# Twelve row slots for two expert tables: four and eight in place of five and seven

## The chip, the cores and the metric

The kernel runs on one core of one Trainium2 chip. The metric is the device time in microseconds of one execution.

## What is computed

Two transformer-like blocks run one after the other on a sequence of 256 tokens of width 1024, all in float32. The part that matters here is the end of the first block, a layer of small experts. For every token and each of 8 heads, a router picks 16 of 16384 experts, so 128 a token; expert k of a token has one row of 1024 numbers in table u and one in table v:

```
def expert_chunk(args):
    xc, ic, gc = args
    u = jnp.take(u_tab, ic, axis=0)
    a = jnp.einsum('chkd,cd->chk', u, xc)
    wgt = gc * jax.nn.gelu(a)
    vv = jnp.take(v_tab, ic, axis=0)
    return jnp.einsum('chk,chkd->cd', wgt, vv)
```

Everything ahead of it (modulation, attention over a window, a short convolution, an output projection) and the whole second block (a state-space mixer, a matrix memory, a feed-forward layer) is untouched by the change.

## The kernel before, in words

**Tiles.** The 256 tokens are two tiles of 128, one token to a partition. The expert layer is a flat sequence of 256 steps, which the text calls experts 0 to 255: 128 for the first tile and 128 for the second. Step e gathers, for each of the 128 tokens, the u row and the v row of that token's expert e: two indirect DMAs of 128 rows of 4 KB, 512 KB each.

**The slots.** The buffer `G` (tile name `gathered`, 12 x 1024 columns) is cut at line 372 into NU + NV = 12 slots: the first NU take u rows in turn (`e % NU`), the other NV take v rows (`e % NV`). NU = 5 and NV = 7 stand in lines 70 and 71. Each slot has a semaphore for its landing (lines 444 and 445). Before the expert layer, other parts of `G` hold attention buffers and a chunk of the output projection's weights (from column 8192 on).

**Who does what.** Five engines work on the steps, each in its own order:

- POOL issues the gathers, in the order u 0, v 0, u 1, then for every e from 1 on u(e + 1), v(e) (lines 678 to 711). `gather_u` waits at line 686 until the dot that last used the slot is done, `gather_v` at line 696 until the pair of sums that holds the slot's last user is done. Sums are counted in pairs: `pairs(n)` is `(n + 1) // 2`, and PE counts only behind every odd expert. POOL works its queue in order, so a u gather that waits also holds up the v gathers behind it, and the other way round.
- DVE multiplies the u row with the token's activation and adds up (`dot_expert`, line 2489, one instruction of 1024 columns), then drains and counts `dot_ready` (line 2491). Between the dots it works through the routing of the experts to come, one piece a step (`route_piece`): it picks the best keys, makes the indices and the gate values of the next 32 experts. A piece can wait for scores that ACT copies out of PSUM.
- ACT makes the weight of the step (`weigh_expert`, lines 1737 to 1746): gelu of the dot, times the gate, spread over a diagonal of 128 x 128. There are 8 diagonals, so expert e waits for the pair with expert e - 8. ACT also copies scores (line 1563) and other PE results in between.
- PE multiplies the diagonal with the v row and adds into two PSUM banks (`sum_expert`, line 1143, two halves of 512 columns, which the profile shows as four matmul records), and has other matmuls laid in between at fixed experts: queries and scores for the router (lines 780 and 1069), and the first products of the second block.
- SP loads weights for these other matmuls.

After expert 255, POOL adds some bias rows and the second block runs.

Of the kernel before, what the change touches and what calls it, by code (L numbers as in the profile page):

```python
# [66 lines left out]
UP_PLACE = {1: (0, 0), 6: (0, 1), 2: (1, 0), 5: (1, 1), 3: (2, 0), 7: (2, 1), 4: (3, 0)}  # L67
UP_BANKS = 4
LAST_PRODUCTS = (1, 6, 2, 5, 3, 7, 4)
NU = 5  # L70
NV = 7
ACC = 4
ROUTE = 2 * TOPK
EXPERTS = HEADS * TOPK
# [170 lines left out]
def pairs(experts):  # L245

    return (experts + 1) // 2


def build(nc, T, out):  # L250

    with ExitStack() as ctx:
# [3 lines left out]
        def sem(name):  # L256
            return ctx.enter_context(nc.semaphore(name))
# [113 lines left out]

        rows = G[:, :].rearrange("p (s n) -> p s n", s=NU + NV)
        u_rows, v_rows = rows[:, 0:NU, :], rows[:, NU:NU + NV, :]
        h2_rows = [psum[:, b:b + 2, :].rearrange("p b n -> p (b n)") for b in H2_BANK]
# [68 lines left out]
        turn_read = sem("turn_read")  # L443
        u_full = [sem(f"u_full{i}") for i in range(NU)]
        v_full = [sem(f"v_full{i}") for i in range(NV)]
        S_ = {}

        def flag(name):

            if name not in S_:  # L450
                S_[name] = sem(name)
            return S_[name]
# [89 lines left out]
        def route_step(e):  # L542

            return e // TOPK if e < ROUTE else e // ROUTE + 1
# [91 lines left out]
        def _(pool):  # L636
# [41 lines left out]
            def gather_u(e):  # L678

                r, k, slot = e // ROUTE, e % ROUTE, e % NU  # L680
                if e in FIRST_IDX:
                    pool.wait_ge(flag("idx_ready"), FIRST_IDX.index(e) + 1)
                elif e == TOPK or (k == 0 and r):
                    pool.wait_ge(flag("idx_ready"), route_step(e) + len(FIRST_IDX))
                if e >= NU:
                    pool.wait_ge(flag("dot_ready"), e - NU + 1)
                pool.indirect_dma_start(  # L687
# [4 lines left out]
            def gather_v(e):  # L692

                r, k, slot = e // ROUTE, e % ROUTE, e % NV
                if e >= NV:
                    pool.wait_ge(flag("pair_summed"), pairs(e - NV + 1))
                if e == 0:
# [2483 lines left out]
```

## Time and profile before

| | us |
|---|---|
| median of 3 runs | 1310.25 |
| lowest and highest of them | 1309.9, 1311.06 |
| span of the profiled execution | 1366.9 |
| time of the profiled execution itself | not given beside its span |
| POOL busy in the span | 500.2 |
| DVE busy | 861.8 |
| PE busy | 1199.9 |

The profile was taken in an execution of its own, which is longer than the runs without one. Times are microseconds from the start of the span. A row of the timeline has the start, the duration, the engine, the line of the kernel, the operation and its tiles, and in brackets how long the engine was idle before it and what ended that. "issue" is idle time that waited for nothing the profile shows, "remote" a releaser that is not on record. DVEq is the sequencer of DVE, which counts a drain. The busy time of POOL holds the issuing of the indirect DMAs, not their transfers.

### The profile page before, as it was taken

The page shows a single profiled execution, that of the slowest core. Times are in us where ns is not written, and L with a number is a line of the kernel's source. Part 1 is how long each engine was busy: PE and PEld are TensorE (multiplying, and loading weights), DVE is VectorE, ACT ScalarE, POOL GpSimd, SP SyncE. Part 2 cuts the span into 40 slices and gives each one's busy share as a digit, 9 for nine tenths or more (in the row PEclk, how much of TensorE's full clock was granted, in tenths as well). Part 3 has the DMA queues.
Part 4 walks back from the last instruction along what each step waited for, and adds up shares of the span by engine and source line. Part 5 has one row for each costly group of instructions (what it writes and reads, how often), then busy time and mean ns, then how long its engine had stood idle before and what let it go on. Part 6 is the DMA issues. An engine that isn't in the chain of part 4 may idle for free. (4 is left out here: it accounts for less than half of the span.)

```text
span 1366.9 us, 14592 instructions
## 1 busy us (share of the span) xinstructions
PE 1199.9 (88%) x4663; PEld 665.4 (49%) x4663; DVE 861.8 (63%) x1765; ACT 420.2 (31%) x1138; POOL 500.2 (37%) x580
## 2 busy tenths in 40 slices
PE   7899888888778978876788889789999999999997
PEld 4676554433344542222345433236544545999443
DVE  2657669574663654776746557679989543676345
ACT  2213334344223343343423324432323311222000
POOL 1000356666665666766666666630000000000000
PEclk9999999999998999999999999999999999999999
DMA  9998789999998999999999999986644444454450
GB/s 358 390 349 326 286 319 339 367 357 367 364 366 300 406 403 405 407 377 364 340 371 353 400 405 409 377 306 233 224 139 148 145 150 156 157 175 145 175 184 31
DMA packets 134303, 405.66 MB, mean 297 GB/s; under 512 B 10153, under 2 KB 11585, under 8 KB 133971
## 3 DMA queue, kind: packets, MB, share of 16 engines
q0 software_dynamic: 75024, 273.19, 53.1%
q1 hardware_dynamic: 57860, 127.48, 25.8%
q10 hardware_dynamic: 1342, 4.06, 0.8%
q8 instruction: 38, 0.62, 0.2%
q14 instruction: 39, 0.31, 0.1%
HBM read 403.12 MB, written 1.05 MB: 296 GB/s over the span
## 5 line engine op out<-in xcount | busy, mean ns | idle before, releaser
L1143 PE MATMUL psum<-gathered,modr 128*128 128x512 f32 x1024 | 505.0, 633 | 130.3 <-DMA gathered<-in_peer_v_dram,expert_idx 49.0
L2489 DVE CUSTOM_DVE_ANT_0 gathered<-gathered,psum 128x1024 f32<-128x1024 f32 x256 | 311.5, 1217 | 202.3 <-DMA gathered<-in_peer_u_dram,expert_idx 153.3
L1143 PEld LDWEIGHTS psum<-gathered,modr 128*128 128x128 f32 x1024 | 190.7, 199 | 404.7 <-issue 284.9
L687 POOL DMA_INDIRECT gathered<-in_peer_u_dram,expert_idx x256 | 244.9, 957 | 240.5 <-DVE expert_idx L1997 144.0
L701 POOL DMA_INDIRECT gathered<-in_peer_v_dram,expert_idx x256 | 242.6, 947 | 169.9 <-remote 73.7
L780 PE MATMUL psum<-featT,weight_ring 128*128 128x128 f32 (+2 forms) x960 | 145.3, 305 | 14.4 <-issue 11.3
L780 PEld LDWEIGHTS psum<-featT,weight_ring 128*128 128x128 f32 x960 | 133.7, 196 | 43.9 <-issue 35.6
L780 PE MATMUL psum<-weight_ring,featT 128*128 128x512 f32 x336 | 147.9, 596 | 1.3 <-ACT featT L1563 0.8
L1737 ACT ACTIVATE gel<-dots 128x1 f32<-128x1 f32 x256 | 51.1, 200 | 255.1 <-issue 128.1
L1746 ACT ACTIVATE modr<-ident,wgt 128x128 f32<-128x128 f32 x256 | 102.8, 402 | 18.5 <-issue 1.1
L780 PEld LDWEIGHTS psum<-weight_ring,featT 128*128 128x128 f32 x336 | 62.6, 190 | 78.8 <-issue 76.6
L1741 ACT ACTIVATE wgt<-gel,expert_gate 128x1 f32<-128x1 f32 x256 | 75.4, 294 | 17.9 <-issue 0.3
L1989 DVE TENSOR_TENSOR work<-work 128x1088 f32<-128x1088 f32 (+5 forms) x87 | 68.6, 801 | 9.6 <-issue 2.8
L725 POOL DMA_DIRECT2D gathered<-in_b_in_dram x6 | 5.3, 942 | 138.6 <-ACT gathered L1585 104.2
L1585 ACT COPY work<-psum 128x128 f32<-128x128 f32 x32 | 8.4, 262 | 81.5 <-remote 44.6
L1978 ACT ACTIVATE work<-work,pack 128x256 f32<-128x256 f32 x28 | 12.7, 500 | 56.8 <-DVE work L1989 56.8
L1989 DVE TENSOR_TENSOR vectors<-weight_ring 128x1024 f32<-128x1024 f32 x14 | 16.5, 1220 | 20.9 <-PE psum L1512 20.9
L1563 ACT COPY featT<-psum 128x512 f32<-128x512 f32 (+1 forms) x24 | 12.4, 554 | 55.0 <-PE psum L752 53.8
L780 PE MATMUL psum<-weight_ring,uT 128*128 128x512 f32 x64 | 28.2, 593 | 1.0 <-ACT gathered L1585 1.0
L1989 DVE TENSOR_TENSOR gathered<-gathered,psum 128x256 f32<-128x256 f32 (+1 forms) x17 | 8.6, 511 | 29.8 <-PE psum L780 24.9
L1473 PE MATMUL psum<-featT,weight_ring 128*128 128x128 f32 x224 | 27.3, 275 | 0.0
L1473 PEld LDWEIGHTS psum<-featT,weight_ring 128*128 128x128 f32 x224 | 26.1, 192 | 0.0
(443 smaller groups left out, 1343.1 us busy)
## 6 DMA issues: line engine op xcount, KB each, us to landing
weight_ring<-in_w_in_dram SPq DMA_DIRECT2D x16, 2048.0 KB
weight_ring<-in_w_up_dram SPq DMA_DIRECT2D x8, 2048.0 KB
weight_ring<-in_w_down_dram SPq DMA_DIRECT2D x8, 2048.0 KB
weight_ring<-in_ada_w_dram SPq DMA_DIRECT2D x5, 2048.0 KB
work<-in_ada_w_dram SPq DMA_DIRECT2D x5, 2048.0 KB, 16.3
weight_ring<-in_peer_wq_dram SPq DMA_DIRECT2D x3, 2048.0 KB
gathered<-in_ada_w_dram SPq DMA_DIRECT2D x2, 2048.0 KB, 14.5
gathered<-in_peer_u_dram,expert_idx POOLq DMA_INDIRECT x256
```

Source lines behind the costliest of these rows:

```text
L687: pool.indirect_dma_start(u_rows[:, slot, :], None, T["peer_u"], bass.IndirectOffsetOnAxis(ap=expert_idx[:, r % 2, k:k + 1], axis=0),).the ...
L701: pool.indirect_dma_start(v_rows[:, slot, :], None, T["peer_v"], bass.IndirectOffsetOnAxis(ap=expert_idx[:, r % 2, k:k + 1], axis=0),).the ...
L780: last = pe.matmul(psum[0:m, bank, 0:n], lhs(k), rhs(k), start=(k == 0), stop=(k == kt - 1))
L1143: mm = pe.matmul(psum[:, SUM_BANK + half, :], diag[:, e % 8, :], v_rows[:, slot, 512 * half:512 * (half + 1)], start=(e % EXPERTS == 0), s ...
L1473: last = pe.matmul(psum[:, UP_BANKS * (n % 2) + bank, at:at + P], a(g, m), b(g), start=(g == 0), stop=(g == 3))
L1563: ins = act.activation(dst, src, func, **kw) if func else act.copy(dst, src)
L1737: act.activation(gel[:, col:col + 1], dots[:, col:col + 1], ACT.Gelu_apprx_tanh)
L1741: act.activation(wgt[:, col:col + 1], gel[:, col:col + 1], ACT.Copy, scale=expert_gate[:, r % 2, k:k + 1])
L1746: act.activation(diag[:, e % 8, :], ident[:, :], ACT.Copy, scale=wgt[:, col:col + 1]).then_inc(flag("diag_full"), 1)
L1978: act.activation(ffT[:, k, :], ffT[:, k, :], ACT.Relu, bias=pk("b_up")[:, k:k + 1])
L1989: return dve.tensor_tensor(o, a, b, op)
L2489: dve.tensor_tensor_reduce(u_rows[:, slot, :], u_rows[:, slot, :], h2_rows[t], 1.0, 0.0, ALU.mult, ALU.add, dots[:, col:col + 1])
```

## The change

The twelve slots are divided four to eight. Nothing else is edited: lines 372, 373, 444, 445, 680, 685, 686, 694 to 696, 1139, 1140, 2485 and 2488 take NU and NV from these two lines.

```
--- before
+++ after
-NU = 5
-NV = 7
+NU = 4
+NV = 8
```

## Rows read from the trace of the kernel before

**Rows 1.** The head of the page

```profile
span 1366.9 us, 14592 instructions
```

**Rows 2.** Windows: us; busy of PE, PEld, DVE, ACT, POOL; PEclk, DMA share, GB/s

```profile
152.00:915.00 763.00, 620.92 (x1844) 298.17 (x1843) 479.45 (x1156) 282.56 (x880) 487.48 (x513) 0.95 0.97 370
...
520.00:580.00 60.00, 51.23 (x103) 18.42 (x102) 38.99 (x102) 21.60 (x70) 40.62 (x43) 0.94 1.03 408
```

**Rows 3.** DMA view, 152 to 915 us: the gathers' queue, packets, MB, share

```profile
q0 software_dynamic: 73728, 268.47, 92.4%
```

**Rows 4.** Timeline, 606 to 617 us: POOL's pace and expert 153

```profile
606.24 0.94 POOL L687 DMA_INDIRECT gathered<-in_peer_u_dram,expert_idx  x1 [0.30 <-issue]
...
608.82 0.94 POOL L687 DMA_INDIRECT gathered<-in_peer_u_dram,expert_idx  x1 [0.30 <-issue]
...
610.07 0.94 POOL L701 DMA_INDIRECT gathered<-in_peer_v_dram,expert_idx  x1 [0.30 <-issue]
...
612.90 1.15 DVE L2489 CUSTOM_DVE_ANT_0 gathered<-gathered,psum 128x1024 f32<-128x1024 f32 x1
...
616.66 1.98 PE L1143 MATMUL psum<-gathered,modr 128*128 128x512 f32 x4 [0.58 <-issue]
```

**Rows 5.** Waits view, POOL: waited for, us in total, times, longest us

```profile
POOL gathered L701 <- remote: 73.7, 29, 4.2
...
POOL gathered L701 <- PE psum L1143: 28.7, 12, 8.7
...
POOL gathered L687 <- DVEq L2491: 23.6, 27, 4.4
```

**Rows 6.** Timeline of POOL, 514 to 535 us: one u gather of the backlog

```profile
527.35 0.94 POOL L687 DMA_INDIRECT gathered<-in_peer_u_dram,expert_idx  x1 [0.38 <-DVEq L2491]
```

**Rows 7.** Timeline: POOL (v 13, v 15, u 17, u 22) and DVE, start

```profile
196.16 0.94 POOL L701 DMA_INDIRECT gathered<-in_peer_v_dram,expert_idx  x1 [1.86 <-PE psum L1143]
...
203.16 0.94 POOL L701 DMA_INDIRECT gathered<-in_peer_v_dram,expert_idx  x1 [2.34 <-PE psum L1143]
...
204.41 0.94 POOL L687 DMA_INDIRECT gathered<-in_peer_u_dram,expert_idx  x1 [0.30 <-issue]
...
218.79 0.94 POOL L687 DMA_INDIRECT gathered<-in_peer_u_dram,expert_idx  x1 [0.30 <-issue]
...
204.52 0.87 DVE L2338 MAX8 work<-work 128x8 f32<-128x128 f32 x4 [9.80 <-ACT work L1563]
...
206.44 0.08 DVE L2489 DVE_READ_ACCUMULATOR2_ANT dots<- 128x1 f32 x1
...
220.55 0.08 DVE L2489 DVE_READ_ACCUMULATOR2_ANT dots<- 128x1 f32 x1
...
251.59 1.22 DVE L2489 CUSTOM_DVE_ANT_0 gathered<-gathered,psum 128x1024 f32<-128x1024 f32 x1 [1.80 <-DMA gathered<-in_peer_u_dram,expert_idx]
```

**Rows 8.** Timeline: POOL (u 88, v 87); two holds of ACT

```profile
408.88 0.94 POOL L687 DMA_INDIRECT gathered<-in_peer_u_dram,expert_idx  x1 [0.30 <-issue]
...
418.52 0.94 POOL L701 DMA_INDIRECT gathered<-in_peer_v_dram,expert_idx  x1 [8.70 <-PE psum L1143]
...
260.50 0.59 ACT L1563 COPY work<-psum 128x512 f32<-128x512 f32 x1 [9.42 <-remote]
...
413.04 0.59 ACT L1563 COPY work<-psum 128x512 f32<-128x512 f32 x1 [15.08 <-remote]
```

**Rows 9.** Timeline of POOL (u 144, v 143) and DVE around 583 us

```profile
580.37 0.93 POOL L687 DMA_INDIRECT gathered<-in_peer_u_dram,expert_idx  x1 [0.30 <-issue]
...
583.55 0.93 POOL L701 DMA_INDIRECT gathered<-in_peer_v_dram,expert_idx  x1 [2.25 <-issue]
...
583.39 0.20 DVE L2384 CAST work<-work 128x64 f32<-128x64 uint32 x1 [4.09 <-issue]
```

**Rows 10.** Timeline of POOL, u 167 and u 168

```profile
645.92 0.94 POOL L687 DMA_INDIRECT gathered<-in_peer_u_dram,expert_idx  x1 [0.30 <-issue]
...
651.76 0.94 POOL L687 DMA_INDIRECT gathered<-in_peer_u_dram,expert_idx  x1 [3.66 <-DVEq L2491]
```

## The prediction

> **What bounds the kernel now.** First the page's head, for the span [rows 1]. The change touches only the stretch in which the two expert tables are gathered, from POOL's first gather at 152 us to the end of the sums near 915 us, so the windows view comes second. In the stretch POOL is busy for 487 of 763 us, DVE for 479, PE for 621, and the DMA engines' share is 0.97 at 370 GB/s; from 520 to 580 us it is 1.03 at 408 GB/s [rows 2]. The reader is to see that no engine is full, that the DMA engines nearly are, and that they can do a tenth more than their mean.
>
> Third, the DMA view: the gathers' queue moves 268.47 MB in the stretch [rows 3]. At 408 GB/s that is 658 us, and one expert (a u row and a v row of 512 KB, 1.05 MB) takes 2.57 us. Fourth, POOL's rows in order of time. A gather holds POOL for 0.94 us and 0.30 us passes before the next, 1.24 us a gather and 2.49 us an expert [rows 4]; 256 experts are 637 us. The rest of the stretch is in POOL's waits: 23.6 us for DVE in front of u gathers (27 times), 28.7 us for PE in front of v gathers (12 times), 73.7 us in which no releaser is on record (29 times) [rows 5]. 637 + 126 is 763; less the 0.30 us counted twice 68 times (20 us) it is 743, and the stretch's last 10 us lie behind the last gather. So POOL's queue sets the pace of the stretch, the DMA engines stand 3% behind it, and a us that POOL is held is a us at the end, except where the DMA engines have a backlog (520 to 580 us: POOL waits 0.38 us for every u slot there [rows 6], and this costs nothing).
>
> The sum is made against one profiled execution with a span of 1366.9 us [rows 1]; the page gives no other time for it. The median of the runs is 1310.25 us, 56.6 us less, so some holds of the trace are surely smaller in the runs, above all those without a releaser. I keep the terms in microseconds and set them on 1310.25.
>
> **The change, part by part.** No instruction is added or removed, and no byte: the same 512 gathers in the same order, 12 slots of the same size, 12 semaphores. Two waits of POOL move. Line 686: u row e waits for dot e-4 in place of e-5. Line 696: pairs(e - 7) in place of pairs(e - 6); for even e both are the pair (e-8, e-7), for odd e it is the pair (e-8, e-7) in place of (e-6, e-5). So every u gather may start one expert (about 2.5 us) less ahead, every odd v gather two experts further ahead, and an even one no further. The v slots move down by 1024 columns; the wait of v 3 for the w_out chunk stays at v 3, where POOL does not wait now; cost nothing, covered by the 0.30 us pace.
>
> Regular flow. Expert 153 [rows 4]: u issued at 606.24, its dot ends at 612.90 + 1.15 = 614.05, 7.8 us later; v issued at 610.07, its sum ends at 618.64, 8.6 us. Five u slots allow 5 x 2.49 = 12.4 us, four 9.96: the slack of a u slot falls from 4.6 to 2.1 us. The odd v row has 6 x 2.49 = 14.9 us now, slack 6.4; with eight slots 7 for even and 8 for odd rows, slack 8.9 at least. While no engine is late both are covered: cost 0. If that cover goes (a dot over 2.1 us late), POOL is held, and v gathers queued behind the u gather, so PE too, are late next. The trade is thus in the holds, and I walk through those of the trace.
>
> (a) Start. POOL counted from its first gather: v 15 waits for PE until 203.16 and u 17 follows at 204.41. With eight v slots v 15 would need only the pair (6, 7), for whose sum v 13 waited until 196.16, and could go at the pace near 199.4; but u 17 then waits for dot 13, which DVE ends at 206.5 after a hold of 9.80 us on the scores [rows 7]. u 17 goes at 206.7, 2.3 us later. Following this on to u 22: it needs dot 18, over at 220.6, and goes at 220.8 in place of 218.79. Cost **+2.0 us**. Is it taken up? At 251.59 DVE stands 1.80 us waiting for a u row [rows 7], so lateness of the stream reaches the dots. Bounds: 0 (taken up by a later hold of POOL) and 2.49.
>
> (b) v 87. ACT is held 15.08 us, until 413.04, the diagonal of expert 81 and its sum are late, and v 87 goes at 418.52 after 8.70 us [rows 8]. With eight slots v 87 needs only the pair (78, 79), a pair earlier than the one that is late: it goes 1.24 us behind u 88 (408.88), at 410.1, u 89 at 411.4, and v 88 waits until 418.5. Two gathers pass before the hold in place of after it: **-2.49 us**. This is the most that one hold on the v side can give.
>
> (c) u 144. DVE is held 4.09 us behind dot 140, until 583.39. u 144 went at 580.37, with four slots it goes at 583.5; v 143, held until 583.55 now, goes at 584.7, the next u at 586.0 in place of 584.8 [rows 9]: **+1.2 us**. Bounds 0 and 2.49.
>
> (d) u 167. u 168 waits 3.66 us for DVE's end of dot 163, until 651.76; with four slots u 167, issued at 645.92 now, is the one that waits [rows 10]. Two gathers fall behind the hold: **+2.5 us** (to 2.9 while DMA restarts).
>
> I counted the other u gathers whose dot e-4 ends after their present issue: they lie in e 4 to 12 and 17 to 24 (in a), at 37 and 38 (1.4 us, inside the 2.0 already carried), and in the stretches in which the DMA engines have a backlog (e 106 to 137, 209 to 212, 224 to 232), where a later issue costs nothing as DMA is full.
>
> Sum: 2.0 - 2.49 + 1.2 + 2.5 = **+3.2 us**; 1310.25 + 3.2 = 1313.4. Nothing behind 915 us changes but its start. With every bound at its low end the sum is -2.49 + 0 + 0 + 0 = -2.5, at its high end without (b) it is 2.49 + 2.49 + 2.9 = +7.9.
>
> A page against this sum: the Trainium skill, "DMA: Bandwidth & Descriptors", section Specifications, gives about 358 GB/s as the limit of one core's HBM reads. By it the gathers alone would take 750 us, the stretch would be bound by bytes, and the change would give 0. The 408 GB/s over 60 us [rows 2] speaks against it here, with one core running.
>
> **The rivals.** *No change.* If the runs lack most of the holds without a releaser (56.6 us are missing in them against 73.7 us of such holds), POOL is ahead of the DMA engines everywhere, the flow is that of 520 to 580 us throughout, and slots only decide how long the backlog is. For it: POOL's 2.49 us is under DMA's 2.57 us. Against: the gap is 0.08 us an expert, so a backlog comes back slowly after a hold. It gives 1310.3 us, up to 2.6 us on either side. The same page, section Anatomy of one DMA, has about 2.0 us plus bytes over 436 GB/s for a gather; by that 512 KB needs 3.2 us, and four slots would be ample.
>
> *Faster.* The v side decides: ACT and PE are held more often or longer than DVE, as at v 87, and each such hold over 6.4 us gives back 2.49 us, while DVE's two holds in (c) and (d), which have no named cause, are not repeated. One such hold: 1307.8 us. ACT has two holds over 9 us in the trace, until 260.50 and 413.04, only the second of which reached POOL [rows 8]; both would give -5.0, 1305.3 us. It decides from the point where PE's sums stand more than 6.4 us behind the flow. Against: the u slots are the tighter ones already.
>
> *Clearly slower.* The slack of 2.1 us is used up by more of DVE's late dots than (c) and (d), since in the runs the flow has a longer backlog and dots end later after issue. Three more at 2.49 us: +10.7, 1320.9 us. Against: the trace has only few DVE holds over 2.1 us after the start.
>
> *The change does nothing to the limits.* Not open: the trace has waits on both semaphores, and both limits come from the two constants.
>
> **How the numbers follow.** Forecast (the sum) 0.44, no change 0.24, faster 0.20, clearly slower 0.12. About 0.2% (2.6 us) is what a measurement of this kernel can tell from nothing; the forecast's own spread, -2.5 to +7.9, puts about a third of its 0.44 inside this, so slower is 0.30 + 0.12 = 0.42, same 0.24 + 0.14 = 0.38, faster 0.20. The range reaches below to the two v holds of the faster rival and a little on (1304.5), above to the clearly slower one (1321).
>
> **What would show it.** In the changed trace POOL's waits for DVE in front of u gathers should grow from 27 times and 23.6 us (many are harmless), those for PE in front of v gathers shrink from 12 times; u 17 should go 2 us later against u 0 and the first u rows be held from u 4 on. A hold of DVE over 2.1 us outside a backlog should hold the very next u gather but three. The stretch from first gather to last should be some 3 us longer at the same count of holds. I am wrong if POOL's wait for DVE doesn't grow, if PE's share of POOL's waits remains with eight v slots, or if the time moves by more than the stretch does.

## Result and profile after

The changed kernel takes 1315.26 us (median of 6 runs, 1314.56 to 1317.41) against 1310.67 us (6 runs, 1309.9 to 1312.61): a ratio of 1.0032, 95% interval 1.0020 to 1.0043. It is slower by 4.2 us, between 2.6 and 5.6. Two more comparisons of the same pair, told below, gave 1.0023 and 1.0036. The largest of the three is under 0.4% of the time.

The page of the changed kernel: its head, three engines' busy rows, and the gathers' queue. The profiled execution's own time is 1314.58 us.

```profile
span 1312.8 us, 14592 instructions
...
PE 1182.7 (90%) x4663; PEld 648.9 (49%) x4663; DVE 866.8 (66%) x1765; ACT 425.5 (32%) x1138; POOL 506.4 (39%) x580
...
q0 software_dynamic: 75024, 273.19, 53.5%
```

The windows view of the same kernel, with the columns of [rows 2]:

```profile
152.00:915.00 763.00, 657.66 (x2185) 317.65 (x2185) 536.07 (x1210) 305.12 (x923) 496.04 (x515) 0.99 0.99 388
520.00:580.00 60.00, 46.41 (x96) 15.95 (x94) 45.06 (x100) 23.47 (x72) 45.27 (x47) 1.00 1.02 407
```

And POOL's waits (waited for, us in total, times, longest us):

```profile
POOL gathered L687 <- DVEq L2491: 84.4, 117, 2.7
...
POOL gathered L701 <- PE psum L1143: 3.0, 10, 0.3
```

Set beside [rows 1, 2, 5] this looks like a gain: the span is 54 us shorter, the 73.7 us of holds without a releaser are gone, and of the 28.7 us for PE 3.0 are left. Since the runs say the opposite, the two profiles cannot be compared directly; first it had to be known which of the two was the odd one.

### The profile page after: what moved, and what is told of

It is laid out like the page before. It is cut to its first block and busy times, and to the rows that moved or that the text cites. A ratio compares the mean times of both kernels' runs of the same rounds, so it can differ in the third digit from the quotient of the medians.

```text
span 1312.8 us, 14592 instructions
## 1 busy us (share of the span) xinstructions
PE 1182.7 (90%) x4663; PEld 648.9 (49%) x4663; DVE 866.8 (66%) x1765; ACT 425.5 (32%) x1138; POOL 506.4 (39%) x580
## 3 DMA queue, kind: packets, MB, share of 16 engines
HBM read 403.12 MB, written 1.05 MB: 308 GB/s over the span
## 5 line engine op out<-in xcount | busy, mean ns | idle before, releaser
L1143 PE MATMUL psum<-gathered,modr 128*128 128x512 f32 x1024 | 494.3, 613 | 105.1 <-DMA gathered<-in_peer_v_dram,expert_idx 93.6
L1143 PEld LDWEIGHTS psum<-gathered,modr 128*128 128x128 f32 x1024 | 179.0, 191 | 383.5 <-DMA gathered<-in_peer_v_dram,expert_idx 231.7
L687 POOL DMA_INDIRECT gathered<-in_peer_u_dram,expert_idx x256 | 251.0, 981 | 271.0 <-DVE expert_idx L1997 144.6
L780 PEld LDWEIGHTS psum<-featT,weight_ring 128*128 128x128 f32 x960 | 130.3, 192 | 28.8 <-issue 20.6
L780 PE MATMUL psum<-featT,weight_ring 128*128 128x128 f32 (+2 forms) x960 | 140.0, 301 | 3.0 <-DVE modr L1989 2.2
L1741 ACT ACTIVATE wgt<-gel,expert_gate 128x1 f32<-128x1 f32 x256 | 75.4, 294 | 17.9 <-issue 0.3
L1473 PEld LDWEIGHTS psum<-featT,weight_ring 128*128 128x128 f32 x224 | 26.1, 192 | 0.0
L1989 DVE TENSOR_TENSOR modr<-weight_ring 128x1024 f32<-128x1024 f32 x14 | 16.5, 1219 | 14.1 <-PE psum L1512 14.1
## 6 DMA issues: line engine op xcount, KB each, us to landing
weight_ring<-in_w_in_dram SPq DMA_DIRECT2D x16, 2048.0 KB, 13.8
```

What stands on the lines that cost most here:

```text
L687: pool.indirect_dma_start(u_rows[:, slot, :], None, T["peer_u"], bass.IndirectOffsetOnAxis(ap=expert_idx[:, r % 2, k:k + 1], axis=0),).the ...
L780: last = pe.matmul(psum[0:m, bank, 0:n], lhs(k), rhs(k), start=(k == 0), stop=(k == kt - 1))
L1143: mm = pe.matmul(psum[:, SUM_BANK + half, :], diag[:, e % 8, :], v_rows[:, slot, 512 * half:512 * (half + 1)], start=(e % EXPERTS == 0), s ...
L1473: last = pe.matmul(psum[:, UP_BANKS * (n % 2) + bank, at:at + P], a(g, m), b(g), start=(g == 0), stop=(g == 3))
L1741: act.activation(wgt[:, col:col + 1], gel[:, col:col + 1], ACT.Copy, scale=expert_gate[:, r % 2, k:k + 1])
L1989: return dve.tensor_tensor(o, a, b, op)
```

## The experiments

Ratios are against runs of the kernel before on the same chip, taken beside the others. Each diff shows only the lines that differ from the kernel before.

**The kernel before, once more.** No edit; one more execution, with a profile.

> The kernel before (five and seven), once more, for a second profile of it. Theory A (the 73.7 us of POOL holds without a releaser, and the long holds of ACT and DVE, belong to the one profiled execution of span 1366.9 us): span near 1309, no POOL wait for 'remote', the stretch of the gathers some 55 us shorter and near 408 GB/s. Theory B (they belong to every profiled execution of this kernel): span near 1365 again.

It took 1312.86 us, a single run. Head of its page, windows, and POOL's waits:

```profile
span 1311.1 us, 14592 instructions
```

```profile
152.00:915.00 763.00, 663.38 (x2191) 321.26 (x2190) 537.81 (x1213) 306.81 (x925) 493.60 (x515) 0.99 0.99 389
```

```profile
POOL gathered L687 <- DVEq L2491: 81.1, 116, 2.4
...
POOL gathered L701 <- PE psum L1143: 4.9, 13, 1.2
```

The difference was that of one execution. Between the gathers there is no wait without a releaser here, and none over 2.4 us: the holds of [rows 8, 9, 10] (ACT's 15.08 us, v 87's 8.70 us, DVE's 4.09 us, u 168's 3.66 us) aren't repeated. Nor is a profiled execution longer as such, as the text on the profile before had it: the thirteen profiled executions after that one lie within 3 us of their kernels' medians. The DMA share over the whole stretch is 0.99 in place of 0.97, as in the backlog of 520 to 580 us. POOL waits for DVE 116 times before the change and 117 times after. This profile, not that of [rows 1 to 10], is what the changed kernel is compared with from here on.

**Where the time goes: the start.** POOL's timeline of the changed kernel: u 4, u 6, u 17, v 16, u 18.

```profile
163.79 0.94 POOL L687 DMA_INDIRECT gathered<-in_peer_u_dram,expert_idx  x1 [2.72 <-DVEq L2491]
...
170.02 0.94 POOL L687 DMA_INDIRECT gathered<-in_peer_u_dram,expert_idx  x1 [1.56 <-DVEq L2491]
...
198.76 0.94 POOL L687 DMA_INDIRECT gathered<-in_peer_u_dram,expert_idx  x1 [0.99 <-DVEq L2491]
200.00 0.94 POOL L701 DMA_INDIRECT gathered<-in_peer_v_dram,expert_idx  x1 [0.30 <-issue]
202.37 0.94 POOL L687 DMA_INDIRECT gathered<-in_peer_u_dram,expert_idx  x1 [1.44 <-DVEq L2491]
```

The same of the kernel before, run again: u 5, u 7, v 15, u 17, u 19.

```profile
164.01 0.94 POOL L687 DMA_INDIRECT gathered<-in_peer_u_dram,expert_idx  x1 [0.30 <-DVEq L2491]
...
170.18 0.93 POOL L687 DMA_INDIRECT gathered<-in_peer_u_dram,expert_idx  x1 [1.51 <-DVEq L2491]
...
195.36 0.94 POOL L701 DMA_INDIRECT gathered<-in_peer_v_dram,expert_idx  x1 [1.18 <-PE psum L1143]
196.60 0.94 POOL L687 DMA_INDIRECT gathered<-in_peer_u_dram,expert_idx  x1 [0.30 <-issue]
...
202.55 0.93 POOL L687 DMA_INDIRECT gathered<-in_peer_u_dram,expert_idx  x1 [1.29 <-DVEq L2491]
```

Counted from the first gather (152.11 and 152.28 us), dot 0 lets u 4 go at 11.7 us after the change; before it u 5 goes at 11.7 us and needs no hold; dot 2 lets u 6 and u 7 go at 17.9; dot 14 lets u 18 and u 19 go at 50.3. The dots come at the same times, but each one admits a u row that stands one place earlier in the queue, so the stream behind it is one expert, two gathers of 1.24 us, late. v 15's wait for PE is gone, as predicted, and gives nothing back: u 17, behind it, now waits for dot 13 and goes at 46.65 in place of 44.32 us.

The dots become late where they begin to wait for rows. DVE's timeline, dot 32 and dot 255, of the changed kernel:

```profile
245.29 1.22 DVE L2489 CUSTOM_DVE_ANT_0 gathered<-gathered,psum 128x1024 f32<-128x1024 f32 x1 [1.33 <-DMA gathered<-in_peer_u_dram,expert_idx]
...
854.88 1.22 DVE L2489 CUSTOM_DVE_ANT_0 gathered<-gathered,psum 128x1024 f32<-128x1024 f32 x1 [0.46 <-DMA gathered<-in_peer_u_dram,expert_idx]
```

and of the kernel before, run again:

```profile
243.22 1.22 DVE L2489 CUSTOM_DVE_ANT_0 gathered<-gathered,psum 128x1024 f32<-128x1024 f32 x1 [1.34 <-DMA gathered<-in_peer_u_dram,expert_idx]
...
853.15 1.22 DVE L2489 CUSTOM_DVE_ANT_0 gathered<-gathered,psum 128x1024 f32<-128x1024 f32 x1 [0.42 <-DMA gathered<-in_peer_u_dram,expert_idx]
```

From the first gather, dot 32 comes at 93.2 against 90.9 us and dot 255 at 702.8 against 700.9: 2.2 us late early on, 1.9 at the end, and over the 223 experts between them the two kernels keep nearly one pace. The windows show why nothing is caught up. Three stretches of the kernel before, run again:

```profile
164.00:197.00 33.00, 30.71 (x125) 17.75 (x124) 25.52 (x68) 15.02 (x46) 22.96 (x25) 1.00 1.02 403
197.00:230.00 33.00, 30.09 (x101) 15.58 (x100) 30.88 (x91) 15.29 (x47) 23.82 (x26) 0.95 1.00 385
230.00:260.00 30.00, 28.34 (x95) 14.23 (x94) 21.03 (x60) 11.75 (x40) 22.68 (x25) 1.00 1.02 406
```

and of the changed kernel:

```profile
164.00:197.00 33.00, 30.71 (x125) 17.82 (x125) 25.62 (x68) 15.14 (x47) 23.57 (x26) 1.00 0.96 361
197.00:230.00 33.00, 30.09 (x102) 15.65 (x101) 30.35 (x89) 15.18 (x46) 23.32 (x25) 0.95 1.01 391
230.00:260.00 30.00, 27.27 (x92) 13.42 (x91) 19.89 (x58) 11.18 (x38) 22.69 (x25) 1.00 1.03 408
```

Last columns: in the first 33 us the DMA engines move 42 GB/s less, 1.39 MB; they regain 6 x 33 and 2 x 30, 0.26 MB. What is left, 1.1 MB, is one expert's two rows (1.05 MB), and at 408 GB/s it is 2.8 us. After that the engines are full in both kernels and cannot win it back. POOL's 117 waits there are no sign of a cost: the kernel before has 116.

The bytes say the same in every profile. In the first 108 us behind the first gather the DMA engines move 41.9 and 42.0 MB in the two profiles with five u slots at the start (the kernel before run again, and u4_from32 below), and 40.8 to 40.9 MB in all eight with four there, or in the start's second half (three of the changed kernel; u4_v8_w7, u4_v7, u4_v7_b, u4_first32, u4_17to31 below). This is firmer than the 1.9 us: u4_from32 runs the same code as the kernel before up to u 32, yet its dot 28 comes 82.2 us after the first gather against 83.3. So one profile's stream is known to about 1 us, and the start's price lies between 1.9 and 3.5 us by the one or the other.

Why a hundred waits behind the start cost nothing shows in how long a gather takes to land. DMA to landing of the gathers, 152 to 850 us, five u slots (the kernel before, run again), then four (u4_v8):

```profile
DMA to landing us min/median/max: 5.0/11.0/19.5
```

```profile
DMA to landing us min/median/max: 4.6/8.5/15.5
```

With the DMA engines full, the time to landing goes with the number of rows under way: one u slot less, 2.5 us less, about what one expert's bytes take. With three u slots the median is 6.1 us. The prediction's slack (the time that the slots allow, less 7.8 us from issue to dot) took this time for fixed.

**Four u slots at the start alone, and after the start alone.** Slots as before, but the u gathers wait for dot e - 4: for e from 4 to 31 (u4_first32), or from 32 on (u4_from32).

```diff
-                if e >= NU:
+                if e >= 4 and e < 32:
+                    pool.wait_ge(flag("dot_ready"), e - 4 + 1)
+                elif e >= NU:
```

> Five and seven slots, but u gathers 4 to 31 wait for dot e-4 as with four slots; all later ones wait for dot e-5. Theory 'start' (the cost is made among the first 20 experts, where DVE and PE are late, and carried to the end): +2.0 to +4 us on the kernel before, and nearly all of the +4.6 us of the whole change. Theory 'spread' (the cost is made by late dots and weight loads all along the stretch): within 1 us of the kernel before.

> Five and seven slots, but u gathers from 32 on wait for dot e-4, the first ones for dot e-5. Theory 'start': within 1 us of the kernel before. Theory 'spread': +3 to +5 us.

At the start alone: 1314.01 against 1312.25 us, 1.0015 (1.0007 to 1.0024). From 32 on alone: 1311.73 us, 0.9992 (0.9984 to 1.0001), no loss. That settles the place: what one u slot less costs is made at 28 of the 256 u rows. It is 2.0 us by these runs, not the whole 3.0 to 4.7 us of the change, as was expected.

The start was then halved, in the same form, with `4 <= e < 17` (u4_4to16) and `17 <= e < 32` (u4_17to31).

> Five and seven, u gathers 4 to 16 wait for dot e-4. In the trace of the kernel before POOL waits 0.88 us at v 15, 0.99 at u 19, 0.43 at u 21 and 0.15 at u 23, 2.45 us in all: these take up the 2.3 us by which the early gathers are late. Taken-up theory: within 0.5 us of the kernel before. If lateness of the first rows counts by itself: +2.3 us.

> Five and seven, u gathers 17 to 31 wait for dot e-4. Taken-up theory: these few waits, the last before the DMA engines are full for good, make the whole cost, +2.3 us. If the first rows count: within 0.5 us of the kernel before.

1.0011 (1.0002 to 1.0020) and 1.0016 (1.0007 to 1.0025) against 1312.29 us. Each half costs, the first by little more than the noise, and they don't add up, as they shouldn't if both buy the same one-expert lateness. For the first half neither no cost nor 2.3 us came true. POOL's timeline of the first half, u 4 and u 17:

```profile
163.82 0.94 POOL L689 DMA_INDIRECT gathered<-in_peer_u_dram,expert_idx  x1 [2.73 <-DVEq L2493]
...
198.10 0.94 POOL L689 DMA_INDIRECT gathered<-in_peer_u_dram,expert_idx  x1 [0.30 <-issue]
```

u 17 goes 46.0 us after the first gather, 1.6 us late, and the waits that the kernel before has at v 15, u 19, u 21 and u 23 take up the rest in POOL's queue. Dot 255 is still 1.0 us late, and 41.6 MB are moved in the first 108 us in place of 41.9: the bytes not asked for early are partly lost. The second half alone loses all of them (40.9 MB).

**Is it the v side after all?** Four u slots and seven v slots, one slot unused (u4_v7, and a second time u4_v7_b), beside the changed kernel again (u4_v8):

```diff
-NU = 5
+NU = 4
...
-        rows = G[:, :].rearrange("p (s n) -> p s n", s=NU + NV)
+        rows = G[:, 0:(NU + NV) * D].rearrange("p (s n) -> p s n", s=NU + NV)
```

> Four u slots, seven v slots, eleven in all: the u side of the change alone. If the eighth v slot is worth nothing (PE is never over 6 us late in an execution without long holds): the same as four and eight, 1315 us, +4.6 on the kernel before. If the eighth v slot gives back what I priced for a hold (2.49 us): 1317 to 1318 us.

> The changed kernel (four and eight) again, beside its own halves on one chip. Start theory: +2 to +4.5 us on the kernel before, as measured first (1.0032), and within 1 us of u4_v7_b.

> Four and seven slots again. The traces of the first four-and-eight and of this kernel agree within 0.1 us at nearly every gather, so the eighth v slot should be worth nothing: the same as u4_v8 within 1 us. If the eighth v slot costs something by itself (as 1.0032 against 1.0011 on two chips could mean), u4_v8 is 2 to 3 us slower than this one.

Eleven slots gave 1.0011 (1.0002 to 1.0020) and 1.0010 (1.0001 to 1.0019); the twelve of the change gave 1.0023 (1.0014 to 1.0032). So the eighth v slot gives nothing back, and against what was expected the two layouts aren't the same: side by side on one chip they took 1315.52 and 1312.99 us. The intervals just overlap, but the changed layout's three comparisons all lie above the two of eleven slots, and the 1.3 to 2.1 us that the start costs by the runs (u4_first32, u4_v7, u4_v7_b, u4_17to31) don't fill them: there is, most likely, a second term.

The eighth slot also relaxes v's waits. The next kernel has four and eight slots, but v waits as with seven (u4_v8_w7), and ran beside the changed kernel a third time (u4_v8_c):

```diff
-NU = 5
-NV = 7
+NU = 4
+NV = 8
...
-                if e >= NV:
-                    pool.wait_ge(flag("pair_summed"), pairs(e - NV + 1))
+                if e >= 7:
+                    pool.wait_ge(flag("pair_summed"), pairs(e - 7 + 1))
```

> Four and eight slots, but every v gather waits for the pair that it would need with seven slots. Tells whether the relaxed v wait does anything: the traces say no, so the same as u4_v8_c within 1 us. If it is 1.7 us faster, the relaxed wait itself costs the difference seen between four-eight and four-seven (1.0023 and 1.0010).

> The changed kernel a third time, beside the one above. Start theory: +2 to +4 us on the kernel before. Its second profile had a hold of 1.8 us behind the gathers (PE near 900 us) that the first one had not; if this belongs to single executions, this profile may show it or not, and the gathers agree with the earlier ones within 0.3 us.

1.0025 (1.0015 to 1.0036) and 1.0036 (1.0024 to 1.0048) against 1311.92 us. Leaving v's waits as they were takes off 0.8 us, which is not clear of the noise, and its profile has the second term in full, so the relaxed waits aren't that term.

**The second term, behind the gathers.** One profile a kernel, us: first gather, from it to dot 255, from there to the end of the span.

| kernel | first gather | to dot 255 | to the end |
|---|---|---|---|
| before, again | 152.28 | 700.9 | 458.0 |
| changed | 152.11 | 702.8 | 457.9 |
| changed, second (u4_v8) | 152.10 | 702.8 | 459.7 |
| changed, third (u4_v8_c) | 152.16 | 702.9 | 459.7 |
| u4_v8_w7 | 152.19 | 702.9 | 461.0 |
| u4_v7 | 151.84 | 703.1 | 458.1 |
| u4_v7_b | 150.37 | 702.7 | 457.9 |
| u4_first32 | 150.44 | 703.1 | 458.1 |
| u4_4to16 | 152.15 | 701.9 | 458.1 |
| u4_17to31 | 152.03 | 703.3 | 458.2 |
| u4_from32 | 152.09 | 699.3 | 457.9 |
| u6_v6 | 152.21 | 701.7 | 461.3 |
| u3_v9 | 152.31 | 721.6 | 459.7 |

The middle column has the start's price: 702.7 to 703.3 us in all eight profiles in which four slots hold at the start, or at its second half, against 700.9 and 699.3 in the two with five. The last is 458 us with seven v slots, and 1.7 to 3.3 us more in five of the six profiles with another number. The row that differs, in PE's timeline near 900 us, is the first products with a weight chunk of the second block; here with the change (u4_v8):

```profile
903.70 0.74 PE L1284 MATMUL psum<-uT,modr 32*128 32x272 f32 x8 [2.08 <-DMA weight_ring<-in_w_in_dram]
```

in the kernel before, run again, and in the changed kernel's first profile:

```profile
899.76 0.74 PE L1284 MATMUL psum<-uT,modr 32*128 32x272 f32 x8
```

```profile
901.50 0.74 PE L1284 MATMUL psum<-uT,modr 32*128 32x272 f32 x8
```

PE is kept waiting for the chunk for 2.08 us. The chunk itself is late. Its transfer was issued at 887.63 us in u4_v8 and at 887.76 us in u4_v7; KB and us to landing, u4_v8 and then u4_v7:

```profile
weight_ring<-in_w_in_dram SPq DMA_DIRECT2D x1, 2048.0 KB, 16.0
```

```profile
weight_ring<-in_w_in_dram SPq DMA_DIRECT2D x1, 2048.0 KB, 13.5
```

What else runs on the DMA engines then is a bias row block that POOL adds (line 725), the second of its kind. POOL's timeline in u4_v8, the copy, the first and the second bias transfer:

```profile
860.94 0.57 POOL L718 DMA_DIRECT2D gathered<-xres  x1 [10.10 <-PE psum L1143]
864.43 0.94 POOL L725 DMA_DIRECT2D gathered<-in_b_in_dram  x1 [2.92 <-DMA gathered<-xres]
895.64 0.86 POOL L725 DMA_DIRECT2D gathered<-in_b_in_dram  x1 [30.27 <-ACT gathered L1585]
```

and the same three in u4_v7:

```profile
861.07 0.57 POOL L718 DMA_DIRECT2D gathered<-xres  x1 [10.33 <-PE psum L1143]
865.78 0.93 POOL L725 DMA_DIRECT2D gathered<-in_b_in_dram  x1 [4.14 <-issue]
896.99 0.86 POOL L725 DMA_DIRECT2D gathered<-in_b_in_dram  x1 [30.28 <-ACT modr L1765]
```

With eight v slots the second bias is issued 1.35 us earlier against an equally late weight stream. That it takes the chunk's place on the DMA engines is argued from these rows and not shown: nobody moved the bias, and the changed kernel's first profile issues it just as early (8.0 us behind the chunk), yet the chunk lands after 13.7 us and PE doesn't wait. The copy is not what differs: it lands 2.9 us after its issue in all of these profiles, and the bias is issued 0.6 us behind the landing with six, eight or nine v slots and 1.8 us behind it with seven. The second bias follows the first by 31.2 us in each. Where the 1.2 us come from stays open.

**The division the other way, and further the same way.** Six and six (w_out's wait stands at v 2, whose slot that chunk holds), and three and nine:

```diff
-NU = 5
-NV = 7
+NU = 6
+NV = 6
...
-                if e == 3:
+                if e == 2:
```

```diff
-NU = 5
-NV = 7
+NU = 3
+NV = 9
```

> One step the other way: six u slots and six v slots; the wait for the w_out chunk moves from v 3 to v 2, which now takes its columns. If the u slots alone set the cost (2.3 us a slot), this should be 2.3 us faster than five and seven: 1310 us against 1312.3. By the rows of the second profile of five and seven the sums take over as the limit at the start: with six v slots v 26 and v 28 would wait 1.0 and 0.8 us longer than they go now, so the start ends within 1 us of five and seven. I expect 1312 to 1313.5 us, no gain.

> The suspected cost doubled: three u slots and nine v slots. If the cost is only the start, another 2.3 to 2.5 us: 1317 us. If three slots no longer cover the time from issue to the end of the dot in the saturated flow (7.8 us in the first trace against 3 x 2.49 = 7.5 us), the whole stretch slows by 0.1 us or more an expert: over 1340 us.

Six and six: 1314.52 us, 1.0023 (1.0014 to 1.0032), a us over what was expected. Three and nine: 1332.54 us, 1.0156 (1.0141 to 1.0170), between the two times that were expected (1317 and over 1340). POOL's waits in six and six, then in three and nine:

```profile
POOL gathered L701 <- PE psum L1143: 67.8, 52, 4.4
```

```profile
POOL gathered L687 <- DVEq L2491: 112.4, 153, 5.2
```

With six v slots the waits move to PE (52 against 13). The stream is only 0.8 us late at dot 255; the other 3.3 us of this profile lie behind it, at the same weight chunk (2.11 us) and beyond. With three u slots u 3 is held already, dot 32 is 6.9 us late (97.8 against 90.9) and dot 255 20.7 us: the start and, here, the rest of the stream too. None of the divisions tried (three, four and six u slots) beats five and seven. A thirteenth slot was not tried.

## Why the prediction was right, and where its reasons were not

**Forecast against measured.** 1313.4 us was forecast, +3.2 us, slower as the most likely side; 1315.26 us, +4.2 by the ratio, was measured, and it is in the range. The size owes something to luck: three of its four terms don't exist in the runs and nearly cancel, and a cost that it lacks stands in for them.

- *What bounds the kernel.* Wrong. "POOL's queue sets the pace of the stretch, the DMA engines stand 3% behind it" was true of one execution whose span was 56 us longer. In the kernel before, run again, the DMA engines are at 0.99 of the stretch. The text's own figures pointed there: 2.57 us an expert for the DMA engines against 2.49 for POOL. The 56.6 us between the span and the runs' median stood in the text, but as a doubt about sizes, where it should have unseated the holds as terms.
- *(a), the start, +2.0.* Right in the wait and nearly in size: u 17 was to go 2.3 us later and went 2.33 us later; dot 255 is 1.9 us late (3.5 beside u4_from32). What carries it to the end is not POOL's pace, as the text had it, but 1.1 MB not moved before the DMA engines are full. The early waits, at u 4 and u 6, were counted in and not walked through; either half of the start costs by itself.
- *(b), v 87, -2.49; (c), u 144, +1.2; (d), u 167, +2.5.* None exists in the runs. They were three walks through holds of a single execution; they sum to +1.2 us, which moved the forecast little only by chance. (The general rule for odd v rows is off by one expert: it is the pair (e-9, e-8) in place of (e-7, e-6). The walks at v 15 and v 87 use the right pairs.)
- *Nothing behind 915 us changes but its start.* Wrong in two of the three profiles: a weight chunk is about 2 us late for PE near 900 us. This is the part of the loss that the forecast lacks. 1.9 us at the start and 1.8 us in two of three profiles, 1.2 us on average, make 3.1 us, and 4.7 us with 3.5 at the start; the three comparisons gave 3.0, 4.2 and 4.7 us, with intervals down to 1.8, 2.6 and 3.1.

**The rivals.** *No change* had the right state of the kernel, DMA full throughout, with the wrong inference: a full DMA keeps a loss of the start, it doesn't heal it. *Faster* needs holds of ACT and PE; 13 waits of at most 1.2 us are left of them, and the v side gives nothing. *Clearly slower* needs a DVE late by more than 2.1 us again and again; behind the start four slots show no loss at all, and only three do (13.8 us between dot 32 and dot 255).

**What was to show it.** u 17 2 us later and the first u rows held from u 4 on: both seen. POOL's waits for DVE were to grow from 27: they are 117, but the like-for-like number before is 116, so this sign was useless, and "I am wrong if POOL's wait for DVE doesn't grow" would have refuted a right term. Waits for PE shrank from 13 to 10. The stretch from first to last gather was to be 3 us longer: it is 4.4 (697.8 against 693.4 us), but there 2.3 us are no loss, as the last rows are merely asked for later; to dot 255 it is 1.9. Against this the time moved by more, which the text took for a sign of being wrong: it is the sign of the term behind the stretch.

**The page against the trace.** The Trainium skill, "DMA: Bandwidth & Descriptors", Specifications, has about 358 GB/s for one core's HBM reads, worked out there as half of what two cores share. The two like-for-like traces move 388 and 389 GB/s over 763 us and 407 and 409 from 520 to 580 us, with one core running, so it is no limit here. What it would have suggested, a stretch bound by bytes, does hold; that the change would then give 0 does not.

## What to carry to other kernels

A stream that keeps the DMA engines full later on is decided while it fills: count how many transfers each queue may have under way before the first consumer reports, and where two streams served by one queue share the slots, look at which one's waits stop the queue first, and try both sides. Here a u slot less costs at the start, the v slot won with it gives nothing back, and one slot moved the other way doesn't pay either. One profile is one execution: where its span and the runs differ by 4%, take a second profile of the unchanged kernel, or trust only those waits that have a reason to be repeated. Compare also what lies behind the part that was changed: about 2 us are lost there in most profiles without seven v slots and in none with seven, though the stream is as late in u4_v7 as in the changed kernel.

## What was not expected of the hardware

- One execution of the kernel before had a span of 1366.9 us with 29 waits of POOL without a releaser (73.7 us) [rows 1, 5]; thirteen later profiles, of this and the other kernels, have none of it.
- The first gather comes at 150.4 us in two profiles and at 151.8 to 152.3 us in the other eleven, with identical work ahead of it. Such a step of nearly 2 us is as large as a term of this study, so a single profile's span can't rank these kernels: u4_v7_b (1311.0) and the kernel before (1311.1) look alike, with streams 1.8 us apart.
- The DMA engines held 403 to 409 GB/s from 520 to 580 us with gathers of 4 KB rows, and 386 to 389 over 763 us (378 with three u slots).
- A gather's time from issue to landing goes with the u slots where the DMA engines are full: in the median 11.0, 8.5 and 6.1 us with five, four and three of them, for the same bytes.
